# Tokens, context and vectors laid out by the host, modulation chunks that pair shift and scale, and a first projection that begins per pair of feature tiles

## The reference

```python
mod = silu(c) @ w_mod + b_mod                 # six vectors of 1024: sh1, sc1, g1, sh2, sc2, g2
mc  = silu(c_ctx) @ w_mod + b_mod             # for the context only mc[0], mc[1] are used
h  = rms_norm(x,   norm1_w) * (1 + sc1) + sh1
hc = rms_norm(ctx, norm1_w) * (1 + mc[1]) + mc[0]
kc, vc = hc @ w_in[:, K], hc @ w_in[:, V]     # context keys and values -> retention states
q, k, v, g, f = split(h @ w_in)               # q and k are rotated (rope) per head
o = bidirectional_retention(q, k, v, states)
...                                           # branches, gate, x = x + g1 * y
x = x + g2 * conv_ffn(modulate(rms_norm(x, norm2_w), sh2, sc2))
```

## Time and profile before

| | us |
|---|---|
| median of 3 runs (2420.99 to 2429.96) | 2428.62 |
| the profiled execution | 2425.04 |
| its span, first to last instruction | 2422.8 |
| busy: PE, PEld | 2275.9, 1487.0 |
| busy: DVE, ACT, POOL | 938.1, 622.0, 150.2 |
| PE's first product of `h` with a weight (L807) | 48.03 |
| PE's first value tile (`vc`) | 102.57 |

### The profile page before, as it was taken

How to read it: one execution, slowest core, us unless ns; L and a number is a source line. 1 busy time by engine, 2 the same in 40 slices (tenths; PEclk the granted TensorE clock), 3 DMA queues, 4 the chain that set the end, 5 groups by cost and what they waited for, 6 DMA issues and landing times.

```text
span 2422.8 us, 25415 instructions
## 1 busy us (share of the span) xinstructions
PE 2275.9 (94%) x10944; PEld 1487.0 (61%) x10944; DVE 938.1 (39%) x1260; ACT 622.0 (26%) x879; POOL 150.2 (6%) x141
## 2 busy tenths in 40 slices
PE   6999999989999999999999997998898989898998
PEld 4874778877888887886678885434343434343433
DVE  4937454558888434596632433010000000000001
ACT  5315233243334226326534211000000000000001
POOL 0222000210000011130000020000000000000000
PEclk8999999999999999999999998999999999999999
DMA  7220344335455332211012237999999999999997
GB/s 277 104 82 9 131 162 161 139 135 183 166 207 210 119 124 104 79 70 36 1 36 104 92 118 300 427 428 427 428 427 428 427 428 427 428 428 427 427 426 303
DMA packets 102358, 571.60 MB, mean 236 GB/s; under 512 B 5774, under 2 KB 28727, under 8 KB 73575
## 3 DMA queue, kind: packets, MB, share of 16 engines
q1 hardware_dynamic: 97328, 523.51, 53.5%
q0 software_dynamic: 3360, 29.56, 3.3%
q10 hardware_dynamic: 1559, 16.91, 1.9%
HBM read 567.86 MB, written 2.10 MB: 235 GB/s over the span
## 4 chain that ended last, share of the span: by engine, by line
PE 36%; DMA 17%; DVE 3%; ACT 1%; issue 1%; SPq 0%; DVEq 0%; ACTq 0%
PE ps L1332 10%; PE ps L807 9%; DMA arena<-in_w_exp_up 8%; PE ps L1432 5%; DMA weights<-in_w_exp_gate 4%; PE ps L1311 3%; DMA arena<-in_w_exp_gate 3%; DVE arena L2115 1%; PE ps L1352 1%; PE ps L1207 1%; PE ps L1187 1%; DMA weights<-in_w_exp_up 1%; DMA weights<-in_w_exp_down 1%; PE ps L1145 1%; PE ps L1164 1%
## 5 line engine op out<-in xcount | busy, mean ns | idle before, releaser
L807 PE MATMUL ps<-weights_r 128*128 128x512 f32 (+1 forms) x2784 | 855.1, 387 | 16.0 <-DVE hT_r L2029 6.7
L807 PEld LDWEIGHTS ps<-weights_r 128*128 128x128 f32 x2784 | 522.0, 189 | 125.4 <-issue 12.4
L807 PE MATMUL ps<-hT_r,weights_r 128*128 128x512 f32 x1264 | 463.8, 391 | 0.0
L1332 PE MATMUL ps<-weights,arena 128*64 128x512 f32 x768 | 354.5, 618 | 59.6 <-DMA weights<-in_w_exp_up 45.1
L1334 PE MATMUL ps<-weights,arena 128*64 128x512 f32 x768 | 355.2, 619 | 0.0
L1332 PEld LDWEIGHTS ps<-weights,arena 128*64 128x64 f32 x768 | 106.3, 142 | 288.4 <-issue 287.1
L2010 DVE TENSOR_TENSOR weights_r<-weights,weights_r 128x4096 fp32r<-128x4096 f32 (+1 forms) x46 | 197.1, 4284 | 206.5 <-ACT weights_r L1517 204.7
L807 PEld LDWEIGHTS ps<-hT_r,weights_r 128*128 128x128 f32 x1264 | 239.1, 189 | 49.6 <-issue 0.5
L807 PE MATMUL ps<-arena_r,weights_r 128*128 128x512 f32 (+1 forms) x640 | 224.2, 386 | 0.0
L1517 ACT ACTIVATE weights_r<-weights 128x4096 fp32r<-128x4096 f32 (+1 forms) x46 | 161.6, 3514 | 193.1 <-PE ps L807 114.9
L2625 DVE TENSOR_TENSOR hT<-hT,ps 128x512 f32<-128x512 f32 x32 | 22.0, 688 | 447.1 <-PE ps L1334 447.1
(11 more groups left out here) (313 smaller groups left out, 2438.1 us busy)
## 6 DMA issues: line engine op xcount, KB each, us to landing
weights<-in_w_exp_gate SPq DMA_DIRECT2D x48, 2048.0 KB, 23.3
weights<-in_w_exp_down SPq DMA_DIRECT2D x42, 2048.0 KB, 28.0
weights<-in_w_exp_up SPq DMA_DIRECT2D x42, 2048.0 KB, 25.9
weights<-in_w_in SPq DMA_DIRECT2D x18, 2048.0 KB, 7.8
arena<-in_w_exp_gate SPq DMA_DIRECT2D x16, 2048.0 KB, 26.8
arena<-in_w_exp_down SPq DMA_DIRECT2D x14, 2048.0 KB, 27.5
arena<-in_w_exp_up SPq DMA_DIRECT2D x14, 2048.0 KB, 28.2
weights<-in_w_up SPq DMA_DIRECT2D x22, 1024.0 KB, 7.4
```

The source lines that it names most:

```text
L807: last = pe.matmul(t, a if w_first else b, b if w_first else a, start=(k == 0 and n == 0), stop=(k == kt - 1 and n == len(pairs) - 1))
L1332: la = pe.matmul(bank(b0 + n)[0:64, :], xe[:, 2 * j + r, 0:64], wa[:, r, n * 512:(n + 1) * 512], start=start, stop=stop)
```

## The change

- The host lays out `x` and the context feature-major (`x`, `ctx_t`), the small vectors as columns (`vectors`), and `w_mod`, `w_in` and `w_up` so that every chunk is one run of 16 KB per partition. PE's transposes of these, and the 18 small transfers, go away. The context is loaded twice, by tokens (for its sums of squares) and by features.
- The square sums of `x` are now made from the feature tiles: ACT squares the even ones, DVE the odd ones, and PE adds over the partitions (`norm(0, "n1", L)`: 8 steps of 4 matmuls with one column).
- Each of the first four modulation chunks holds 256 shift and 256 scale columns, so that chunk c gives all that feature tiles 2c and 2c+1 need. `first_tiles` begins after chunk 0; the modulation steps and turns for chunks 1 to 3 stand between its steps (`after`).
- PE's order becomes: `qk1` 0 to 3, `qk1` 4, `spread(1, "nc")`, `qk1` 5 to 7, `kc`. On DVE and ACT all 8 ropes stand ahead of `prepare(("in1", 1))`, and `kc` and its decayed copies behind it. The context's norm is computed behind the split of `("in1", 1)`.
- `row_silu(silu_rows2)` moves from the squares of `n2` to behind the split of `("up", 1)`; the first `mod_sum` of the up projection stands ahead of its loop; the four double chunks come one step later.

```diff
-            + [("mod2", c) for c in (4, 0, 5, 1, 6, 2, 7, 3, 8, 9, 10, 11)])
+            + [("mod2", c) for c in (4, 5, 0, 6, 1, 7, 2, 8, 3, 9, 10, 11)])
@@ sync
-            sp.dma_start(cst[:, :], consts).then_inc(S["consts_in"], 16)
+            sp.dma_start(xT[:, :, :], x).then_inc(S["x_in"], 16)
-            early_load("x")
-            for n in range(NCH):
+            first_in1 = chunk_at["in1", 0]
+            for n in [first_in1] + [n for n in range(NCH) if n != first_in1]:
@@ tensor
-            turn("vecs", [(i * P, rows_v[0:r, i, :]) for i, r in enumerate((104, 88, 88, 104))])
-            w = slot(landed(pe, "x"), TT)
-            for k in range(KT):
-                turn(("xT", k), [(t * P, w[:, t, k * P:(k + 1) * P]) for t in range(TT)])
             pe.wait_ge(S["ones_ready"], 4)
+            norm(0, "n1", L)
             pe.wait_ge(S["silu_ready"], 2)
             mod_step("mod1", 0)
-            spread(0, "n1", L)
-            for c in range(1, 4):
-                mod_step("mod1", c)
-            mod_turn("mod1", 3)
-            w = slot(landed(pe, "ctx"), TT)
-            for k in range(KT // 2):
-                turn(("cT", k), [(j * LC + t * P, w[:, t, (2 * k + j) * P:(2 * k + j + 1) * P])
-                                 for j in range(2) for t in range(CT)])
+            mod_turn("mod1", 0)
+            mod_step("mod1", 1)
+            first_tiles(("in1", 0), [("qk1", i) for i in range(4)], h_parts, "h_ready", 0,
+                        after={0: lambda: mod_turn("mod1", 1), 1: lambda: mod_step("mod1", 2),
+                               2: lambda: mod_turn("mod1", 2), 3: lambda: mod_step("mod1", 3),
+                               4: lambda: mod_turn("mod1", 3)})
+            feature_tiles(("in1", 1), [("qk1", 4)], h_parts)
             spread(1, "nc", LC)
-            first_tiles(("in1", 0), [("qk1", i) for i in range(4)], h_parts, "h_ready", 0)
+            feature_tiles(("in1", 1), [("qk1", 4 + i) for i in range(1, 4)], h_parts, c0=P)
             pe.wait_ge(S["h_ready"], 16)
             token_tiles(("in1", 1), [("kc", t) for t in range(CT)], hc_parts)
-            feature_tiles(("in1", 1), [("qk1", 4 + i) for i in range(4)], h_parts)
@@ scalar
             for i in range(4):
                 rope_raw("qk1", i, i, raw, DK ** -0.5)
+            for i in range(4, 8):
+                rope_raw("qk1", i, i, raw, 1.0)
             prepare(("in1", 1))
             for t in range(CT):
                 copy_out(("kc", t), kc[:, t, :])
-            for i in range(4, 8):
-                rope_raw("qk1", i, i, raw, 1.0)
             prepare(("in1", 2))
@@ vector
+            for k in range(1, KT, 2):
+                ve.tensor_tensor(squares(0, k), xT[:, k, :], xT[:, k, :], ALU.mult).then_inc(S["sq_odd"], 1)
             norm_recip(0, "n1", L)
             norm_scale(0, "n1", xT, hT, L)
-            mod_columns("mod1", 0)
-            mod_columns("mod1", 1)
             prepare(("mod1", 1))
-            mod_columns("mod1", 2)
-            mod_columns("mod1", 3)
-            mod_scales("mod1", (0, 1))
+            for c in range(PE_MODS):
+                mod_columns("mod1", c)
+                first_scales(c)
+                for k in (2 * c, 2 * c + 1):
+                    low_h(0, k, *h_parts, hT)
+            prepare(("in1", 0))
             norm_recip(1, "nc", LC)
...
             for i in range(4):
                 rope_halves("qk1", i, i, rope_cs, raw, rsin, rcos, obuf[:, 2 + 2 * i, :])
+            for i in range(4):
+                rope_halves("qk1", 4 + i, 4 + i, rope_cs, raw, rsin, rcos, obuf[:, 3 + 2 * i, :])
             prepare(("in1", 1))
             wait_freed(ve, ("kc", CT - 1))
...
-            for i in range(4):
-                rope_halves("qk1", 4 + i, 4 + i, rope_cs, raw, rsin, rcos, obuf[:, 3 + 2 * i, :])
@@ up projection
-                    row_silu(silu_rows2, 3)
+            row_silu(silu_rows2, 3)
+            mod_sum("mod2", UP_MODS[0])
             for j in range(UPN):
...
-                        mod_sum("mod2", UP_MODS[j])
+                        if j:
+                            mod_sum("mod2", UP_MODS[j])
```

More of the change, by code:

```diff
@@ L403, in in1 @@
         def in1(i):
-            chunk(("in1", i), kmaj(w_in[0], 512 * i, 512 * i + 512))
+            chunk(("in1", i), w_in[i])
         mod1(0)
@@ L820, in feature_tiles, with first_tiles @@
                     fill(tn, last)
-            def first_tiles(cname, tnames, x, sem, ready, kt=KT, between=None):
+            def first_tiles(cname, tnames, x, sem, ready, kt=KT, after=None):
                 w = parts_of(cname, kt)
@@ L832, in first_tiles @@
                             fill(tnames[n], last)
-                    if between and k == kt // 2 - 1:
-                        between()
+                    if after and k in after:
+                        after[k]()
             def token_tiles(cname, tnames, src, c0=0, width=512, t0=0):
@@ L1295, in expert_chunk @@
                 sl = m % ESLOTS
-                loads = sum(queued_parts(n) for n in range(sl, NCH, RAW)) if sl < RAW else int(sl < SLOTS)
+                loads = sum(queued_parts(n) for n in range(sl, NCH, RAW)) if sl < RAW else int(sl in [i for i, _ in early.values()])
                 pe.wait_ge(S[f"landed{m % ESLOTS}"],
@@ L1610, in _ @@
             mod_silu()
-            x_tok = slots[landed(act_e, "x")][:, :].rearrange("p (t d) -> p t d", t=TT)
-            x_sums = small[:, 60:64]
+            A(small[:, 4:5], eps_col, ACT.Sqrt)
+            act_e.wait_ge(S["x_in"], 16)
             for k in range(0, KT, 2):
-                last = token_squares(x_tok, x_sums, (k // 2,))
-                if k == KT - 2:
-                    last.then_inc(S["x_squared"], 1)
-                copy_out(("xT", k), xT[:, k, :])
-            act_e.wait_ge(S["x_squared"], 1)
@@ L1630, in _, with first_mod @@
-            norm_affine(0, hT, L, lambda k: scale_a[:, 0, k:k + 1], lambda k: mod_cols[:, k, 0:1],
-                        h_parts[0], 0)
-            for k in range(2, KT // 2):
-                copy_out(("cT", k), hc[:, 2 * k:2 * k + 2, :].rearrange("p a b -> p (a b)"))
-            prepare(("in1", 0))
+                A(squares(0, k), xT[:, k, :], ACT.Square).then_inc(S["sq_even"], 1)
+            norm_root(0, "n1", L)
+            prepare(("mod1", 1))
+            def first_mod(c):
+                mod_rows("mod1", c)
+                act_e.wait_ge(S["first_mods"], c + 1)
@@ L2852 @@
     tensors["w_mod_rows"] = rows_of_outputs(tensors["w_mod"])[PE_MODS:]
-    tensors["w_mod"] = np.ascontiguousarray(tensors["w_mod"][:, :, 0:512 * PE_MODS])
+    first = tensors["w_mod"][0, :, 0:512 * PE_MODS].reshape(D, 2, PE_MODS, 256).swapaxes(1, 2)
+    tensors["w_mod"] = chunks_of_columns(first.reshape(D, 512 * PE_MODS))
+    tensors["w_in"] = chunks_of_columns(tensors["w_in"][0])
+    up = tensors["w_up"].reshape(D, 2, UPN, 256).swapaxes(1, 2)
+    tensors["w_up"] = chunks_of_columns(up.reshape(D, 2 * FFN))
+    tensors["vectors"] = vector_columns(tensors)
+    tensors["x"] = rows_by_partition(tensors["x"][0].T)
+    tensors["ctx_t"] = rows_by_partition(tensors["ctx"][0].T)
+    tensors["w_mod_rows"] = tensors.pop("w_mod_rows")
+    for name in VECTORS:
+        del tensors[name]
     for name, a in tensors.items():
```

196 lines of the change are left out of this document (91 added, 105 removed), and 1 row of the table last_tile.

## The result

| | us |
|---|---|
| kernel before, median of 4 runs (2420.99 to 2430.72) | 2429.29 |
| changed kernel, median of 4 runs (2455.12 to 2460.08) | 2458.66 |
| ratio, with its 95% interval | 1.0118 (1.0105 to 1.0130) |
| profiled executions, before and after | 2425.04, 2460.08 |
| PE's first product of `h`, before and after | 48.03, 43.89 |

The change makes the kernel 29.4 us slower. The forecast was slower, 2446, with a range up to 2457; the time lies 1.7 us outside. The two profiled executions differ by 35.0: that of before is 4.3 under its median, that of after the slowest of its four.

A forecast was written before the change was run, and what follows sets the result against it. The prediction took one chain into the experts as the bound, so a microsecond in the first stage moves the end by one. 2425.04 + 27.1 (head) - 7.6 (up projection) = 2444.5, taken as 2446; range 2431 to 2457.

The forecast's parts named there:

- step 5: Ropes on DVE: eight take 36.2 us ahead of the third chunk's split; first value tile at 127.2, 24.6 us later.
- step 3 and 4: First projection's tiles, second chunk's split: of 12 us only 2 left, PE waits 0.7 and 2.3, keys end 1 us later.
- step 1: Start of the first norm: x, vectors and constants, 2.59 MB, pass by 9.0 us, table loads hidden behind the transfer.
- step 2: Norm to first product: norm takes 11.3 us (bounds 7.6 and 15.0), first product at 36.0, 12 us earlier.
- step 6: Norm n2 and up projection: earlier last square and no 4.34 us split wait, -7.6 us, bounds -3 and -9.
- Rival (a): First norm, first step and ropes: quicker or earlier, net +2 to +11, 2428 to 2439 us; chance 0.22.
- Rival (b): Third chunk's split done before 108, ahead of PE's need: head start kept, 2413 to 2414 us; chance 0.09.
- Rival (c): Up gain only 3 and norm cold throughout, or moved key work uncovered: 2452 to 2458 us; chance 0.11, shared.

The follow-up runs named there:

- the warmed run: Changed kernel with the constants first and 20 unused 128 by 128 products on PE from about 1.3 us, ahead of the norm: 2451.18 us.
- the up edits: Kernel before with only the edits around the second norm and up projection (modulation chunk order, Silu of the rows, first modulation sum): 2423.56 us, ratio 0.9973.

## Why the prediction was right in its mechanism and too low in its size

| step | forecast | measured | off by |
|---|---|---|---|
| 1: norm starts | 9.7 | 14.67 | +5.0 |
| 2: norm takes | 11.3 | 13.8 | +2.5 |
| 2: norm's end to first product | 15.0 | 15.4 | +0.4 |
| 3, 4: first product to the end of the context's spread | 40.3 | 41.6 | +1.3 |
| 5: from there to the first rope on DVE | 10.2 | 10.2 | 0 |
| 5: eight ropes | 36.2 | 36.1 | -0.1 |
| 5: first value tile | 127.2 | 136.3 | +9.1 |
| 6: norm n2 and up projection (this pair of executions) | -7.6 | -5.2 | +2.4 |

**Right.** The decisive step was step 5, and it was right to the tenth: eight ropes take 36.1 us, the split ends behind them, PE stands idle for 23.6 us where I had said 24, and the value tiles run slowly behind it (1.9 us, where I had 2.5). Moving that one split gives back 27 us in the changed kernel and costs 12.3 in the kernel before. PE's waits of 0.44 for feature tile 6 and of 2.03 for the second chunk's split stand where step 3 and 4 put them (0.7 and 2.3). The moved key work and the fourth split cost nothing: PE has no wait among the value products. The layout of `w_in` and `w_up` alone is worth nothing. One reading was too wide: DVE is nearly as full as PE from 48 to 102.5 us (48.3 of 54.5), but not among the value products (33.90 of 71.50 in the earlier trace rows).

**Wrong, step 1.** This is the largest term that failed: the bounds allowed 0.3 more, and it took 5.0 more. I counted 2.59 MB through one pipe, so that vectors, constants and `x` land together at 9.0. `x` did (8.2 us after its issue; at 9.29 with the constants first). But the bytes in front were not shared out fairly: ACT's queue with 2 KB runs got a tenth beside SP's 16 KB runs, and went on getting a tenth while the weights came behind `x`. The sum of bytes says when the last of **all queued** transfers lands, not when a given one does. It cost twice: with the vectors there only at 9.15 to 9.20 the table loads no longer hid behind the transfer, and ACT's first square was ready near 12.9; then the constants held the norm until 14.67. The term cost 5.0 us: constants first gave back 5.3. That the squares don't need the vectors at all, and the norm only its column of ones, which POOL writes, and no constants, would have been seen from the code.

**Wrong, step 2.** For the clock of the norm I took half and half, 11.3 of 7.6 to 15.0, and its records were slow throughout, 13.8, three times out of three. The bound covered it, the choice didn't. The earlier trace rows had shown such products at 0.95 us for a tile, but with wide products in front of them; in the first stage there were none. The granted clock of the windows reads 1.00 all through this norm though its records took 0.215 us each, as against 0.10 in the fast part of the warmed run, so that column would not have told it either.

**Short, steps 3 and 4.** The 1.3 us are mostly a slow pace that the sum left out: behind the 2.03 us pause the 24 products of `qk1` 4 took 7.2 us (77.73 to 84.92), not 5.4.

**Too high, step 6.** The 4.34 us wait went, as forecast. But the double chunks left PE waiting 1.73, 0.71, 0.59 and 1.08 us, against 0.50, 0.68 and 0.41 for the three in the kernel before: 2.5 us came back where the sum had 0.5. The norm in front gave 0.7, where I had 1.2. The bounds (-3, -9) held it. All this is one pair of executions. From the first load for the up projection to the first for the down projection the three profiled kernels without the up edits take 266.1, 267.7 and 268.8 us, the eleven with them 259.0 to 263.2, and the medians of the up edits alone say 6.4. So 5.2 is a low reading, and that step 6 was too high is not sure.

**The sum again with what was measured**: 33.75 for the value tiles, about 2 of slow clock behind them and 1.3 more up to the up projection, less 5.2, is 31.9; the medians say 29.4, with 25.5 to 31.6 from the interval. Against the forecast's 19.5 (27.1 - 7.6) that is 8.6 more in the head (9.1 at the first value tile, 0.6 less of slow clock behind it), 1.3 behind it and 2.4 in the up projection.

Rival (a) asked for quicker or earlier ropes; they took 36.1 and began 9.3 later than in my sum. Rival (b) asked for a split that ends before 108; it ended at 136.3. Rival (c) had the cold norm and the smaller up gain, +8.4 together, and named 2452 to 2458: it was the nearest, for half of its reason. The norm did cost 2.5 more and the up edits gave 2.4 less in this pair, but the largest miss, the late constants, was in no case. That the time came so near to (c) is in part luck.

**What stays open.** The 1.3 us between the value products and the up projection lie between the loads of `w_four_out` and `w_ret_out`. They look like the spread of executions: from the issue behind the value tiles (171.97 before) to the load of `w_ret_out` the fourteen profiled executions take 234.2 to 238.3 us, before 234.7, after 236.0, and the layout alone 238.3, in no order of what was edited. The runs with the third split ahead of all ropes and after rope 0 differ by 7 us in the medians and by nothing in the spans of their profiled executions (both 2429.9). The first of these is the fastest of its ten, 6.8 under its median, the second stands at its median; so the equal spans say little. The traces show 4.4 us at the value tiles and 1.7 at the first load for the down projection (755.23 and 753.54), and what makes it 7 in the medians is not settled. What brings the clock down in the middle of the norm is open too.

## What to carry to other kernels

When an edit moves work in time, follow the in-order engine that serves the next stage: a head start of 4 us on PE's first product was worth nothing at the value tiles because steps and turns of the modulation had moved in between the tiles and a 4.4 us split stood behind 36 us of ropes on DVE, and placing that one split anew was worth 27 us. Put small transfers that something early waits for ahead of the large ones on the same queue, not beside them on another. And where an unknown is bounded by two rows, take the row whose surroundings are like the new place (what the engine did before), not the middle.

## What was unexpected of the hardware

- Beside a queue of 16 KB runs a queue of 2 KB runs moved its 0.50 MB from about 3 to 14.6 us, at some 43 of 426 GB/s. With 2 KB runs on both, they were there 4.8 us after the issue.
- The clock fell from 2.4 to 1.2 GHz in the middle of 64 narrow products that followed one another (granted clock 1.00 at 12 to 14 us, 0.54 at 14 to 16, 0.50 after), though PE counted as busy all the time; its last pause, of 1.10 us, had ended 4 us earlier.
- Before the first fall of the clock in these executions the granted clock of the windows reads 1.00 even where records take twice their fast time (0.215 us in the changed kernel's norm against 0.10 in the warmed run). The length of a record is the better witness there.
- Table loads: ACT's first operation with a new table began 0.01 to 0.02 us behind the load (9.20 + 1.28, then 10.50). The Trainium skill ("ScalarE: Activation LUTs", section "What ACT_TABLE_LOAD costs") has a drain of 1.38 us there; this trace disagrees, as that of before did.
